# Four edits in one two-block kernel: head sums in one-pass form, tail by token halves, table rows on two queues, filter taps ahead of splits

## The chip, the cores and the metric

One Trainium2 chip, one core. The metric is device time in microseconds (us) of one execution of the whole program. The profiled execution is one more run of the same program with the hardware profiler on.

## The reference, cut to what matters

Two blocks are applied to x, 256 tokens of 2048 channels, all in float32. The first has two layers of attention plus spatial gating, and a convolution-gated feed-forward part. The second block (`second_block`) modulates by a conditioning vector and mixes the tokens in two branches: a long convolution (Hyena) and a state-space scan (SSD). It ends with a squared-ReLU MLP and a final norm. The pieces that the change touches are these.

```python
# filter of the long convolution, per channel and order
h = h * jnp.exp(-t[:, :, None, None] * jnp.abs(deltas))
k = jnp.concatenate([h[:, :, 0], zeros, h[:0:-1, :, 1]], axis=0)
k = k / (jnp.sum(jnp.abs(k), axis=0, keepdims=True) + EPS)
return jnp.fft.rfft(k, axis=0)

# within a chunk of 128 tokens, per head (16 heads, two directions)
cs = jnp.cumsum(a, axis=-1)
diff = cs[..., :, None] - cs[..., None, :]          # segsum, lower triangle
cb = jnp.einsum('bclgn,bcsgn->bgcls', cc, bc)
y_diag = jnp.einsum('bgcls,bgrcls,bcsgrp->bclgrp', cb, jnp.exp(segsum(a)), xdt)

# the end of the program
x = x + g2 * (jnp.square(jax.nn.relu(h @ w1)) @ w2)
return x * lax.rsqrt(jnp.mean(x * x, axis=-1, keepdims=True) + EPS) * final_norm_w
```

## The kernel before, in words

The core's time is a long row of products of 256 tokens with weights that stream from HBM. A weight piece is four tiles of 128x512. SP loads it in two halves into one of four slots (`w_raw`). ScalarE rounds it to float32r (`w_hi`, a form that TensorE takes in one pass), VectorE forms the remainder (`w_lo`), and TensorE runs three matmuls for each tile and token half: high by high, high by low, low by high. All five engines run orders written out by hand. What sets them against each other are semaphores: `w_loaded`, `w_hi`, `w_lo` and `w_free` for the slots, `t_full` and `t_free` for the two PSUM banks `turn0` and `turn1`, `side_full` and `side_free` for the banks `side0` and `side1`, `acc_free` for the four accumulator banks.

**Start.** Before the first product the per-channel vectors of layer 0 must be turned into columns. `table_rows(0)` names nine DMAs of rows into `staged`: two of 16 rows, three of 8 rows, then `conv_b` and three of `conv_w` of 88 rows each. ScalarE's queue issues all of them (L908), behind three for `cond_rows` (L904, L905), and TensorE's `turn_tables` waits for all nine. SP meanwhile issues `ident`, the first quarter of x and the first weight pieces. TensorE turns two quarters of x (`turn_x`) before the first product.

**Filters.** The filter of the long convolution is made in eight steps, `FLT_A` and `FLT_B` giving the slots (a slot is one weight piece of the second block). In slot FLT_A[s] TensorE writes the raw filter to the side banks. VectorE then runs `filter_taps(s)` one slot later, in `filter_step`, after `split_lo2(n + 2)`, the remainder for the piece two slots ahead, or after the `ada_last` sums (`c_sums`) where that piece is one of `w_ada`. TensorE, at the end of its slot FLT_B[s], waits for `flt_taps` and writes the norm (L2600) and the transform (L2605). `filter_spectrum(s)` on VectorE reads them. SP stores the result with two DMAs into `k_store`, and the taps of the next step wait for these (`k_stored`). The step s = 1 lies in the loop ahead of the slots, s = 0 too.

**Heads.** For each of the 16 heads VectorE's `head_steps` scales masks by the step sizes into `dlh` (four instructions). TensorE's `head_sums` multiplies `dlh` as stationary operand with a triangle of `masks` as moving operand: four float32 matmuls of 128 columns for each of two directions. ScalarE exponentiates each direction (L1217, in a loop), VectorE multiplies by `cbm` (L1973), and TensorE's `head_outputs` runs six small matmuls (L2685). TensorE's order is sums of head h + 1, outputs of head h, sums of head h + 2, and so on, with two buffers of each kind.

**Tail.** In the last quarter of the MLP, `gated_add(1, p, c)` adds the gated product of column quarter c to x, ScalarE's `x_squares2` sums its squares. After the last quarter come `x_norm`, a root on GpSimd, eight multiplications by root and weight (L2172) and eight DMAs to `out` on SP's queue.

The instructions for one matmul slot are these:

```python
nc.tensor.matmul(o, h_[:, kt, tok], wh[:, k, 0:cols], start=(kt == first), stop=False)
nc.tensor.matmul(o, h_[:, kt, tok], wl[:, k, 0:cols], start=False, stop=False)
last = nc.tensor.matmul(o, l_[:, kt, tok], wh[:, k, 0:cols], start=False, stop=(kt == final))
```

## Time and profile before

| what | value |
|---|---|
| device time, median of 3 runs | 3502.82 us (3501.29 to 3503.66) |
| the profiled execution's own time | 3501.27 us |
| its span in the trace | 3499.5 us |
| TensorE busy (PE) | 3407.4 us, 97% |
| VectorE busy (DVE) | 2373.2 us, 68% |
| ScalarE busy (ACT) | 1618.5 us, 46% |
| mean granted TensorE clock | 0.991 of full |
| HBM read | 689.15 MB, 199 GB/s over the span |

Busy shares are averages over stages. TensorE is nearly always busy, so a stage's time is TensorE's own work plus the places where it waits. PE rows are matmul records, PEld rows are weight loads. A plain float32 matmul leaves two records, a float32r one leaves one. The printed length of a record holds its way through the array, so that neighbours overlap; the distance of two starts is the better price. SPq and ACTq rows are the issue of DMAs on these queues.

### The profile page before, as it was taken

How to read it: one execution, taken by the hardware profiler on the slowest of the kernel's cores; microseconds unless marked ns; L12 is line 12 of the kernel's file. 1: busy time of each engine (PE TensorE's matmuls, PEld its weight loads, DVE VectorE, ACT ScalarE, POOL GpSimd, SP SyncE). 2: the span in 40 equal slices, each digit the busy share in tenths (PEclk: the TensorE clock that was granted, in tenths of full speed). 3: DMA queues.
4: the chain of work that ended last, by engine and by line, in shares of the span. 5: the costliest groups of instructions: out<-in, count | busy, mean ns of one | idle time of the engine just before them, and what ended most of it. 6: DMA issues, size and time to landing. Idle time of an engine off the chain costs nothing.

```text
span 3499.5 us, 43122 instructions
## 1 busy us (share of the span) xinstructions
PE 3407.4 (97%) x15842; PEld 2805.7 (80%) x15842; DVE 2373.2 (68%) x2974; ACT 1618.5 (46%) x2146; POOL 32.5 (1%) x28
## 2 busy tenths in 40 slices
PE   8999999999999999999999999999999999999998
PEld 6888888887778888888887887777866788888886
DVE  5667888888666666777777676676676655556565
ACT  5555555455334555555555444234432544444443
POOL 0000000000000000000000000000000000000000
PEclk9999999999999999999999999999999999999999
DMA  7557777776677557777777773346603566666664
GB/s 256 147 178 222 222 224 228 228 223 217 223 227 222 150 177 220 223 228 232 233 229 239 256 247 113 101 150 198 216 19 127 168 215 207 210 207 214 200 221 156
DMA packets 369459, 697.56 MB, mean 199 GB/s; under 512 B 25487, under 2 KB 37792, under 8 KB 368672
## 3 DMA queue, kind: packets, MB, share of 16 engines
q1 hardware_dynamic: 368628, 695.25, 62.9%
q8 instruction: 101, 1.65, 0.2%
q14 instruction: 46, 0.38, 0.0%
q10 hardware_dynamic: 684, 0.28, 0.0%
HBM read 689.15 MB, written 6.29 MB: 199 GB/s over the span
## 4 chain that ended last, share of the span: by engine, by line
PE 64%; issue 22%; DVE 6%; DMA 3%; ACT 2%; DVEq 2%; ACTq 0%; POOL 0%; SPq 0%; POOLq 0%
PE acc L2185 16%; PE acc L2187 16%; PE acc L2186 16%; PE acc L2473 3%; PE acc L2475 3%; PE acc L2474 3%; DMA w_raw<-in_w_down 2%; DVE w_lo L1320 2%; PE turn L2395 1%; DVE ada_sum L1424 1%; PE turn L2206 1%; PE turn L2222 1%; ACT w_hi L825 1%; DVEq L1416 1%; PE acc L2685 1%
## 5 line engine op out<-in xcount | busy, mean ns | idle before, releaser
L1320 DVE TENSOR_TENSOR w_lo<-w_raw,w_hi 128x1024 fp32r<-128x1024 f32 x708 | 838.4, 1221 | 372.9 <-ACT w_hi L825 336.2
L825 ACT ACTIVATE w_hi<-w_raw 128x1024 fp32r<-128x1024 f32 x708 | 739.0, 1062 | 718.2 <-DMA w_raw<-in_w_up 317.4
L2185 PE MATMUL acc<-w_hi,in_h 128*128 128x512 f32 x1408 | 552.7, 393 | 0.0
L2187 PE MATMUL acc<-w_hi,in_l 128*128 128x512 f32 x1408 | 548.6, 390 | 0.0
L2186 PE MATMUL acc<-w_lo,in_h 128*128 128x512 f32 x1408 | 548.1, 389 | 0.0
L2124 DVE TENSOR_TENSOR w_lo<-w_raw,w_hi 128x1024 fp32r<-128x1024 f32 x252 | 303.4, 1223 | 196.1 <-ACT w_hi L1284 186.3
L1284 ACT ACTIVATE w_hi<-w_raw 128x1024 fp32r<-128x1024 f32 x252 | 265.0, 1060 | 332.2 <-DMA w_raw<-in_w_mlp 331.6
L2473 PE MATMUL acc<-w_hi,in_h 128*128 128x512 f32 x992 | 394.7, 398 | 8.4 <-DVE in_l L2100 4.3
L2474 PE MATMUL acc<-w_lo,in_h 128*128 128x512 f32 x992 | 388.3, 391 | 0.8 <-issue 0.8
L2475 PE MATMUL acc<-w_hi,in_l 128*128 128x512 f32 x992 | 388.5, 392 | 0.0
L1424 DVE SCALAR_TENSOR_TENSOR ada_sum<-w_raw,silu_c,ada_sum 128x512 f32<-128x512 f32 x450 | 327.6, 750 | 31.0 <-issue 7.0
L2185 PEld LDWEIGHTS acc<-w_hi,in_h 128*128 128x128 f32 x1408 | 264.4, 188 | 56.0 <-issue 1.7
L2187 PEld LDWEIGHTS acc<-w_hi,in_l 128*128 128x128 f32 x1408 | 264.3, 188 | 55.3
L2186 PEld LDWEIGHTS acc<-w_lo,in_h 128*128 128x128 f32 x1408 | 264.5, 188 | 53.4
L2185 PE MATMUL acc<-w_hi,ah 128*128 128x512 f32 x704 | 279.5, 397 | 14.5 <-DVE w_lo L1320 8.5
L2187 PE MATMUL acc<-w_hi,al 128*128 128x512 f32 x704 | 276.6, 393 | 0.0
L2186 PE MATMUL acc<-w_lo,ah 128*128 128x512 f32 x704 | 276.4, 393 | 0.0
L2473 PEld LDWEIGHTS acc<-w_hi,in_h 128*128 128x128 f32 x992 | 187.7, 189 | 49.9 <-issue 11.2
L2475 PEld LDWEIGHTS acc<-w_hi,in_l 128*128 128x128 f32 x992 | 187.5, 189 | 41.1 <-issue 1.2
L2474 PEld LDWEIGHTS acc<-w_lo,in_h 128*128 128x128 f32 x992 | 187.6, 189 | 38.1 <-issue 0.7
L2473 PE MATMUL acc<-w_hi,hid_h 128*128 128x512 f32 x512 | 200.3, 391 | 0.0
L2475 PE MATMUL acc<-w_hi,hid_l 128*128 128x512 f32 x512 | 199.3, 389 | 0.0
(365 smaller groups left out, 4714.6 us busy)
## 6 DMA issues: line engine op xcount, KB each, us to landing
w_raw<-in_w_up SPq DMA_DIRECT2D x352, 512.0 KB, 3.8
w_raw<-in_w_mlp SPq DMA_DIRECT2D x256, 512.0 KB, 3.7
w_raw<-in_w_in SPq DMA_DIRECT2D x200, 512.0 KB, 3.7
w_raw<-in_w_ada SPq DMA_DIRECT2D x192, 512.0 KB, 4.2
w_raw<-in_w_down SPq DMA_DIRECT2D x176, 512.0 KB, 5.0
w_raw<-in_w_o SPq DMA_DIRECT2D x64, 512.0 KB, 3.7
w_raw<-in_w_out SPq DMA_DIRECT2D x32, 512.0 KB, 3.9
K<-k_store SPq DMA_DIRECT2D x16, 256.0 KB, 6.5
```

The costliest lines, as they stand in the source:

```text
L825: nc.scalar.activation(hi[s][:, ks], raw[s][:, ks], ACT.Copy).then_inc(w_hi[s][h], 1)
L1284: nc.scalar.activation(hi[s][:, 2 * h:2 * h + 2], raw[s][:, 2 * h:2 * h + 2], ACT.Copy).then_inc(w_hi[s][h], 1)
L1320: nc.vector.tensor_tensor(lo[s][:, ks], raw[s][:, ks], hi[s][:, ks].bitcast(F32), ALU.subtract).then_inc(w_lo[s][h], 1)
L1416: dve.drain()
L1424: a = nc.vector.scalar_tensor_tensor(ada_sum[v][:], raw[s][:, k], c, ada_sum[v][:], ALU.mult, ALU.add)
L2124: nc.vector.tensor_tensor(lo[s][:, ks], raw[s][:, ks], hi[s][:, ks].bitcast(F32), ALU.subtract).then_inc(w_lo[s][h], 1)
L2185: nc.tensor.matmul(acc[p][i][:], high(kt)[:, tok], hi[s][:, k], start=(kt == first), stop=False)
L2186: nc.tensor.matmul(acc[p][i][:], high(kt)[:, tok], lo[s][:, k], start=False, stop=False)
L2187: last = nc.tensor.matmul(acc[p][i][:], low(kt)[:, tok], hi[s][:, k], start=False, stop=(kt == final))
L2473: nc.tensor.matmul(o, h_[:, kt, tok], wh[:, k, 0:cols], start=(kt == first), stop=False)
L2474: nc.tensor.matmul(o, h_[:, kt, tok], wl[:, k, 0:cols], start=False, stop=False)
L2475: last = nc.tensor.matmul(o, l_[:, kt, tok], wh[:, k, 0:cols], start=False, stop=(kt == final))
```

## The change

It has four parts.

1. **Table rows on two queues.** SP issues the last four of the nine table DMAs, behind `ident` and ahead of x, once `staged` is cleared. ScalarE's queue keeps the first five.
2. **Filter taps ahead of splits.** `filter_step` falls in two: `filter_first` (the taps) runs ahead of `split_lo2` or of the `ada_last` sums of its slot, `filter_second` (the spectrum) where both stood.
3. **Heads.** The triangle is the stationary operand and the scaled mask moves. All are float32r: the step sizes are split once into `da_h` and `da_l`, VectorE makes `dlh` from `da_h`, ScalarE makes `dll` from `da_l` (four more activations for each head, `low_steps`). Each direction takes two matmuls of 384 columns and two of 128. ScalarE's loop over heads is written out, and three masks are copied to float32r (`masks_r`).
4. **Tail.** The last two pieces of the MLP run for token half 0 first and then for half 1 (`last_rows`). Each half has its own add, square sum, root and output. Columns 0 to 1535 are multiplied by the norm weight beforehand (`x_g`); ScalarE applies the root to part of them and issues two of the output DMAs on its own queue.

```diff
@@ constants
-    c["masks"] = np.stack([k <= q, k > q, k + q >= 0, k < q, k >= q], 1).astype(f32)
+    c["masks"] = np.stack([k <= q, k + q >= 0, k >= q, k > q, k < q], 1).astype(f32)
@@ buffers
-    dlh = [sbt(f"dlh{i}", [P, 2, 3 * P], at=at(3 * i)) for i in range(2)]
+    dlh = [sbt(f"dlh{i}", [P, 2, 3 * P], F32R, at(3 * i)) for i in range(2)]
+    dll = [sbt(f"dll{i}", [P, 2, 3 * P], F32R, at(24 + 3 * i)) for i in range(2)]
...
@@ sync
         sp.dma_start(ident[:], t["ident"]).then_inc(ident_in, 16)
+        sp.wait_ge(staged_clear, 1)
+        for dst, src in table_rows(0)[5:]:
+            sp.dma_start(dst, src).then_inc(staged_in, 16)
         x_chunk(0)
...
-        for i in range(TT):
-            for c in range(4):
-                sp.wait_ge(final_s, 4 * i + c + 1)
-                sp.dma_start(out[0, i * P:(i + 1) * P, c * CH:(c + 1) * CH], x_sb[:, i, c * CH:(c + 1) * CH]).then_inc(stored, 16)
+        for i, c in ((0, 3), (0, 0), (0, 1), (0, 2), (1, 3), (1, 2)):
+            sp.wait_ge(*(((final_a, c + 1) if i == 0 and c < 3 else (final_s, (1 if i == 0 else 5 - c)))))
+            src = x_sb[:, i, c * CH:(c + 1) * CH] if c == 3 else x_g[:, i, c * CH:(c + 1) * CH]
+            sp.dma_start(out[0, i * P:(i + 1) * P, c * CH:(c + 1) * CH], src).then_inc(stored, 16)
@@ gpsimd
-        root(22, x_rstd[:], x_ss[:], TT)
+        for i in range(TT):
+            root(22 + i, x_rstd[:, i:i + 1], x_ss[:, i:i + 1], 1)
@@ scalar
-        for dst, src in table_rows(0):
+        for dst, src in table_rows(0)[:5]:
...
+                    act_.wait_ge(dft_in, 48)
+                    for i, m in enumerate((1, 3, 4)):
+                        a = nc.scalar.activation(masks_r[:, i], masks[:, m], ACT.Copy)
+                    a.then_inc(masks_s, 1)
...
-        for g in range(2):
-            with act_.Fori(0, 4) as hp:
-                for m in range(2):
-                    h = act_.snap(hp * 2 + (8 * g + m))
...
+        def low_steps(h, m):
+            step = lambda i, d: da_l[:, i, ds(h + d * NH, 1)].bitcast(F32)
+            nc.scalar.activation(dll[m][:, 0, 0:2 * P], masks[:, LE:ONES + 1].rearrange("p m q -> p (m q)"), ACT.Copy, scale=step(0, 0))
+            nc.scalar.activation(dll[m][:, 0, 2 * P:], masks[:, LE], ACT.Copy, scale=step(1, 0))
+            nc.scalar.activation(dll[m][:, 1, 0:2 * P], masks[:, ONES:GE + 1].rearrange("p m q -> p (m q)"), ACT.Copy, scale=step(1, 1))
+            nc.scalar.activation(dll[m][:, 1, 2 * P:], masks[:, GE], ACT.Copy, scale=step(0, 1)).then_inc(dll_s, 1)
...
+        for m in range(2):
+            low_steps(m, m)
+        for h in range(NH):
+            exponentials2(h, h % 2)
+            if h + 2 < NH:
+                low_steps(h + 2, h % 2)
...
+        for i in range(TT):
+            act_.wait_ge(x_up, 8 + i)
+            square_sum2(x_sb[:, i, 3 * CH:], x_parts[:, i, 3:4]).then_inc(x_sq, 1)
+            act_.wait_ge(gained_s, 3)
+            act_.wait_ge(rstd, 22 + i)
+            for c in range((3, 2)[i]):
+                ch = slice(c * CH, (c + 1) * CH)
+                nc.scalar.activation(x_g[:, i, ch], x_g[:, i, ch], ACT.Copy, scale=x_rstd[:, i:i + 1]).then_inc(final_a, 1)
+                if i == 1:
+                    act_.wait_ge(final_a, 4 + c)
+                    nc.scalar.dma_start(out[0, P:, ch], x_g[:, 1, ch]).then_inc(stored, 16)
@@ vector
+            nc.vector.tensor_copy(da_h[:], dt_da[:])
+            dve.drain()
+            nc.vector.tensor_tensor(da_l[:], dt_da[:], da_h[:].bitcast(F32), ALU.subtract)
...
         for j in range(12):
             for n, s in pieces_of(j):
+                if n > 0:
+                    filter_first(n)
                 if n + 2 in ADA2:
...
                 if n > 0:
-                    filter_step(n)
+                    filter_second(n)
...
+                if last and n in (20, 24, 29):
+                    c = (n - 20) // 4
...
+                    nc.vector.tensor_tensor(x_g[:, :, ch], x_sb[:, :, ch], f_norm[:, ch].unsqueeze(1).to_broadcast([P, TT, CH]), ALU.mult).then_inc(gained_s, 1)
...
+        for i in range(TT):
+            dve.wait_ge(rows_done, i + 1)
+            nc.vector.tensor_tensor(res_t[1][:, i], acc[1][i][:], g_rows[1][:, ch], ALU.mult)
+            dve.drain()
+            nc.vector.tensor_tensor(x_sb[:, i, ch], x_sb[:, i, ch], res_t[1][:, i], ALU.add).then_inc(x_up, 1)
+            dve.wait_ge(x_sq, 63 + i)
+            nc.vector.tensor_reduce(x_ss[:, i:i + 1], x_parts[:, i], X_AXIS, ALU.add)
...
+            dve.wait_ge(rstd, 22 + i)
+            nc.vector.scalar_tensor_tensor(x_sb[:, i, ch], x_sb[:, i, ch], x_rstd[:, i:i + 1], f_norm[:, ch], ALU.mult, ALU.mult).then_inc(final_s, 1)
+        nc.vector.tensor_scalar(x_g[:, 1, 2 * CH:], x_g[:, 1, 2 * CH:], x_rstd[:, 1:2], None, ALU.mult).then_inc(final_s, 1)
@@ tensor, head_sums
-                own = ((0, 0), (2 * P, P)) if d == 0 else ((P, 0), (2 * P, 2 * P))
-                across = P if d == 0 else 0
-                for at_, l0 in own:
-                    nc.tensor.matmul(tb[b][:, at_:at_ + P], w[:, d, l0:l0 + P], masks[:, near], start=True, stop=True)
-                part = 2 * P if d == 0 else P
-                nc.tensor.matmul(tb[b][:, across:across + P], w[:, d, 0:P], masks[:, ONES], start=True, stop=False)
-                last = nc.tensor.matmul(tb[b][:, across:across + P], w[:, d, part:part + P], masks[:, near], start=False, stop=True)
+                across = (P, 0)[d]
+                for w in (dlh[m], dll[m]):
+                    nc.tensor.matmul(tb[b][:, 0:3 * P], masks_r[:, 1 + d], w[:, d], start=(w is dlh[m]), stop=False)
+                for w in (dlh[m], dll[m]):
+                    last = nc.tensor.matmul(tb[b][:, across:across + P], masks_r[:, 0], w[:, d, 2 * P:], start=False, stop=(w is dll[m]))
@@ tensor
+        def last_rows(p):
+            for i in range(TT):
+                tok = slice(i * P, (i + 1) * P)
+                for n in (30, 31):
...
+                last.then_inc(rows_done, 1)
```

Three places in the order of the instructions. The first is VectorE in slot 13, the last filter step, where the piece two slots ahead is one of `w_ada`. Before:

```order
L1408 SCALAR_TENSOR_TENSOR ada_last_156<-w_raw_59,silu_c,ada_last_156 128x512 [waits w_loaded3_1]
L1408 SCALAR_TENSOR_TENSOR ada_last_156<-w_raw_59,silu_c,ada_last_156 128x512
L1844 TENSOR_TENSOR flt_h_199<-side,flt_decay 128x512 [waits side_full1,side_full0]
L1845 SCALAR_TENSOR_TENSOR flt_q<-side,not_first_sb,flt_decay 128x256
L1846 TENSOR_TENSOR flt_q<-side,flt_decay 128x256
L1850 TENSOR_TENSOR flt_sum<-flt_h_199,flt_q 128x512 [waits k_stored]
```

And now:

```order
L1898 TENSOR_TENSOR flt_sum<-flt_h_204,flt_q 128x512 [waits k_stored]
L1899 TENSOR_TENSOR flt_dif<-flt_q,flt_h_204 128x512
L1901 TENSOR_TENSOR flt_q<-flt_sum,flt_dif 128x512
L1902 TENSOR_TENSOR flt_h_204<-flt_sum,flt_dif 128x512
L1904 SCALAR_TENSOR_TENSOR flt_q<-flt_h_204,flt_q 128x512
L1449 TENSOR_SCALAR ada_last_156<-w_raw_59,silu_c 128x512 [waits w_loaded3_0]
L1451 SCALAR_TENSOR_TENSOR ada_last_156<-w_raw_59,silu_c,ada_last_156 128x512
L1451 SCALAR_TENSOR_TENSOR ada_last_156<-w_raw_59,silu_c,ada_last_156 128x512 [waits w_loaded3_1]
L1451 SCALAR_TENSOR_TENSOR ada_last_156<-w_raw_59,silu_c,ada_last_156 128x512
L1911 TENSOR_SCALAR flt_r<-turn 128x256 [waits t_full1]
```

The taps moved ahead of the four sums, and the four sums now stand between taps and spectrum.

The second is ScalarE in the heads. Before, a pass of the loop is one load of the exponential table and two heads (the numbers behind the names are buffers):

```order
L1217 ACT_TABLE_LOAD
L1217 ACTIVATE decays_196<-turn 128x384 [waits t_full0]
L1217 ACTIVATE decays_196<-turn 128x384 [waits t_full1]
L1215 REGISTER_ALU
L1216 REGISTER_ALU [waits mt_used]
```

And now, two heads in a row:

```order
L1239 ACTIVATE decays_202<-turn 128x384 [waits t_full0,mt_used]
L1239 ACTIVATE decays_202<-turn 128x384 [waits t_full1]
L1227 ACTIVATE dll_197<-masks_sb,da_l 128x256
L1228 ACTIVATE dll_197<-masks_sb,da_l 128x128
L1229 ACTIVATE dll_197<-masks_sb,da_l 128x256
L1230 ACTIVATE dll_197<-masks_sb,da_l 128x128
L1239 ACTIVATE decays_201<-turn 128x384 [waits t_full0,mt_used]
```

Four activations from SBUF came in between the exponentials of one head and of the next, and the table is loaded once.

The third is the end of ScalarE's order, where nothing but the square sums stood before:

```order
L1133 ACTIVATE junk_242,x_parts<-x_sb 128x512 [waits x_up]
L1351 ACTIVATE x_g<-x_g,x_rstd 128x512 [waits rstd,gained_s]
L1354 DMA out<-x_g 128x512 [waits final_a]
L1351 ACTIVATE x_g<-x_g,x_rstd 128x512
L1354 DMA out<-x_g 128x512 [waits final_a]
```

These are the rows of token half 1: a square sum, and two copies with a DMA issue behind each.

## Rows read from the trace of the kernel before

**Rows 1.** TensorE's longest wait: in total, times, longest, us
```profile
PE turn L2600 <- DVEq L1857: 11.7, 6, 3.8
```

**Rows 2.** Timeline of the start: start us, us, engine, what, idle before
```profile
5.34 1.40 ACTq L908 DMA_DIRECT2D staged<-in_conv_w x3
...
13.72 1.30 PE L2206 MATMUL turn<-ident_sb,staged 128*128 128x128 f32 x5 [4.92 <-DMA staged<-in_conv_w]
...
20.09 0.77 PE L2185 MATMUL acc<-w_hi,n_h 128*128 128x512 f32 x1
```

**Rows 3.** DMA issues in the first 45 us: KB each, median us to landing
```profile
ident_sb<-in_ident SPq DMA_DIRECT2D x1, 64.0 KB, 1.8
...
cond_rows<-in_b_ada ACTq DMA_DIRECT2D x1, 48.0 KB, 5.9
```

**Rows 4.** DMA issues from 2.6 to 3.1 us: the second quarter of x
```profile
x_sb<-in_x SPq DMA_DIRECT2D x1, 512.0 KB, 8.0
```

**Rows 5.** Timeline of TensorE at the filter steps
```profile
2210.61 1.13 PE L2600 MATMUL turn<-flt_q,masks_sb 128*128 128x256 f32 x4 [0.66 <-DVEq L1857]
...
2268.75 2.07 PE L2600 MATMUL turn<-flt_q,masks_sb 128*128 128x256 f32 x4 [3.54 <-DVEq L1857]
...
2320.71 1.13 PE L2600 MATMUL turn<-flt_q,masks_sb 128*128 128x256 f32 x4 [1.47 <-DVEq L1857]
...
2325.66 0.40 PE L2504 MATMUL side<-ident_sb,dt_T 32*128 32x32 f32 x4 [2.08 <-DVE flt_h L1869]
```

**Rows 6.** Timeline of VectorE at the filter steps, slots 9 and 13
```profile
2261.11 2.35 DVE L1759 TENSOR_TENSOR w_lo<-w_raw,w_hi 128x1024 fp32r<-128x1024 f32 x2
...
2311.69 0.48 DVE L1406 TENSOR_SCALAR ada_last<-w_raw,silu_c 128x512 f32<-128x512 f32 x1 [8.13 <-PE acc L2491]
...
2317.20 0.69 DVE L1850 TENSOR_TENSOR flt_sum<-flt_h,flt_q 128x512 f32<-128x512 f32 x1 [0.62 <-DMA k_store<-flt_dif]
```

**Rows 7.** Windows: length, busy PE, PEld, DVE, ACT, POOL, then granted clock, DMA
```profile
2261.00:2272.00 11.00, 7.46 (x33) 6.13 (x32) 8.11 (x13) 0.00 (x0) 0.00 (x0) 0.84 0.45 132
...
2531.30:2579.00 47.70, 47.54 (x424) 47.25 (x423) 28.06 (x72) 19.93 (x38) 0.00 (x0) 1.00 0.17 58
```

**Rows 8.** Timeline of TensorE in the heads
```profile
2549.25 1.45 PE L2685 MATMUL acc<-xdt,decays 128*128 x12
...
2550.54 0.66 PE L2672 MATMUL turn<-masks_sb,dlh 128*128 128x128 f32 x4
...
2552.38 1.45 PE L2685 MATMUL acc<-xdt,decays 128*128 x12
```

**Rows 9.** Timeline of TensorE: float32r matmuls of 256 columns in a row
```profile
2288.12 0.28 PE L2475 MATMUL acc<-w_hi,hc_l 128*128 128x256 f32 x1
2288.24 0.28 PE L2473 MATMUL acc<-w_hi,hc_h 128*128 128x256 f32 x1
```

**Rows 10.** Windows: the last 11 us of TensorE, 512 columns each
```profile
3475.00:3486.00 11.00, 10.96 (x49) 8.74 (x47) 1.81 (x3) 0.00 (x0) 0.00 (x0) 1.00 0.00 0
```

**Rows 11.** Groups of instructions: one by form, xcount, busy us, mean ns
```profile
L1272 ACT ACTIVATE in_h<-n_f,mod 128x256 fp32r<-128x256 f32 x16 | 7.2, 500 | 5.4 <-DVE n_f L2109 5.4
```

**Rows 12.** Timeline of ScalarE behind the heads
```profile
2577.59 0.49 ACT L1217 ACTIVATE decays<-turn 128x384 f32<-128x384 f32 x1 [0.40 <-PE turn L2675]
2577.98 2.43 ACT L1220 ACTIVATE g_diag<-ident_sb,mod 128x128 f32<-128x128 f32 x8
```

**Rows 13.** Timeline of the tail
```profile
3486.00 1.29 DVE L2081 TENSOR_TENSOR res_t<-acc,g_rows 128x512 f32<-128x512 f32 x2 [9.19 <-PE acc L2475]
...
3488.63 0.63 ACT L1123 ACTIVATE junk<-x_sb 128x512 f32<-128x512 f32 x1 [16.25 <-DVE x_sb L2084]
...
3491.40 5.39 DVE L2172 SCALAR_TENSOR_TENSOR x_sb<-x_sb,x_rstd,f_norm 128x512 f32<-128x512 f32 x8 [0.81 <-POOL x_rstd L794]
...
3492.18 4.97 SPq L785 DMA_DIRECT2D out<-x_sb x8
```

**Rows 14.** DMA issues in the last 10 us: KB each, us to landing
```profile
out<-x_sb SPq DMA_DIRECT2D x8, 256.0 KB, 2.2
```

More of the change, by code:

```diff
@@ L1296, in hidden @@
                     a.then_inc(acc_free[p], 1)
-                if last and n >= 16 and n % NS == 3:
+                if last and n >= 16 and n % NS == 3 and n < 31:
                     x_squares2(4 + (n - 16) // NS + 1, (n - 16) // NS)
@@ L1946, in _ @@
         block_scales((2,))
-        LE, GT, ONES, LT, GE = range(5)
+        LE, ONES, GE, GT, LT = range(5)
         for g in range(2):
@@ L2135, in hidden @@
                         sl, r = ring(mlp_product(n), q)
-                        dve.wait_ge(w_free[sl][1], r + 1)
-                        if last:
+                        if not (last and c == 3):
+                            dve.wait_ge(w_free[sl][1], r + 1)
+                        if last and c < 3:
                             gated_add(1, p, c)
+                        elif last:
+                            continue
                         else:
@@ L2686, in head_outputs @@
             last.then_inc(mt_used, 1)
+        pe.wait_ge(masks_s, 1)
         head_sums(0, 0)
@@ L2791, in _ @@
         last.then_inc(side_full[0], 1)
+        def last_rows(p):
+            for i in range(TT):
+                tok = slice(i * P, (i + 1) * P)
+                for n in (30, 31):
+                    s, r = ring(mlp_product(n), 3)
+                    for k in range(4):
+                        kt = 4 * (n - 28) + k
+                        if k % 2 == 0:
+                            pe.wait_ge(w_lo[s][k // 2], r)
+                        nc.tensor.matmul(acc[p][i][:], hid_h[:, kt, tok], hi[s][:, k], start=False, stop=False)
+                        nc.tensor.matmul(acc[p][i][:], hid_h[:, kt, tok], lo[s][:, k], start=False, stop=False)
+                        last = nc.tensor.matmul(acc[p][i][:], hid_l[:, kt, tok], hi[s][:, k], start=False, stop=(kt == KT - 1))
+                last.then_inc(rows_done, 1)
         def hidden(q, last_q):
@@ L2823, in hidden @@
                     n = 16 + NS * c + s
+                    if last_q and n >= 30:
+                        if n == 30:
+                            last_rows(p)
+                        continue
                     product2(mlp_product(n), 4 * s, [(p, hid_h, hid_l, CH)], q)
```

55 lines of the change are left out of this document (35 added, 20 removed).

## The prediction, made before the changed kernel had run

> **What bounds the kernel now.** I read the waits of TensorE first, then the timelines around each of them, then the windows for the granted clock. TensorE works nearly all of the span, so an edit pays only where it shortens TensorE's own work or a wait of TensorE, or what lies before its first and after its last product. The four parts of the change sit at four such places. At the start nothing can be multiplied before nine rows of tables have landed [rows 2]. At the filter steps TensorE waits six times for VectorE's taps [rows 1, 5]. In the heads TensorE is full, and its records are short [rows 8]. After the last product 13.5 us pass, from 3486.0 to the end of the span at 3499.5 [rows 13]. The rest of the kernel, some 3,350 us of products, keeps its instructions and should take what it took.
>
> **Start.** The last table DMAs are issued on ScalarE's queue from 5.34 to 6.74; TensorE turns the rows at 13.72, and the first product starts at 20.09, 6.4 us behind [rows 2]. So the rows land some 7 us after their issue, where `ident`, first in its queue and alone, took 1.8 us and `b_ada`, issued at about 2.2 behind three large loads on SP, took 5.9 [rows 3]. In the changed kernel SP issues the four rows of 88 first, from about 1.9 (the memset of `staged`) to 3.7, so they land before its large loads start. What is left on ScalarE's queue ends with a DMA that was issued at 4.6. Priced like `b_ada`, which had as many large loads ahead of it, it lands at 10.5; priced like `ident`, at 6.4. I take 9.5, nearer to `b_ada`: 4.2 us sooner. The price is that all of SP's loads start 2.5 us later (four issues and the wait). The second quarter of x landed at 2.71 + 8.0 = 10.7 [rows 4] and will at 13.2; TensorE turns it 4.3 us behind the tables, at 13.8, so it just hides. If the tables came sooner still, this quarter would be late next, and the gain ends at 5 us.
>
> The Trainium skill, "DMA: Bandwidth & Descriptors", section "Issuing engines are not separate DMA queues", speaks against this: starting DMAs from several engines saves only the time of issuing them. Here the time of issue is 1.8 us (the last DMA of ScalarE's queue ends at 5.0 in place of 6.74), and by the rule that would be the gain. No row shows a queue with the rows ahead of the large loads.
>
> **Filter taps.** The taps take 5.3 us (from the end of two remainders at 2263.4 to TensorE's start at 2268.75) and the two remainders ahead of them 2.3 us [rows 5, 6]. Six waits come to 11.7 us [rows 1]. Two of them, 1.7 and 3.8 us, belong to the steps ahead of the slots, whose order stays. The four others are 0.66 in slot 5, 3.54 in slot 9, a like one of 0.6 in slot 11, and 1.47 in slot 13 [rows 5]. With the taps 2.3 us earlier the small ones go (1.2 us) and slot 9 keeps 1.3, because there VectorE comes late from the convolution taps: 2.3 us off. In slot 13 nothing is gained: the taps stood still for the store into `k_store` until 2317.20 [rows 6], a DMA that SP issues when TensorE has finished its slot, so they end at 2320.6 as before. And something is lost: the four `ada_last` sums, 3.2 us from 2311.69 [rows 6], ran while TensorE wrote the raw filter and the store was under way. Now they stand between the taps and the spectrum, start at 2320.7 and end at 2323.9, where the spectrum started at 2321.9. TensorE's wait for the spectrum's second product grows from 2.1 to 4.1 us [rows 5]. Net: 1.2 + 2.3 - 2.0 = 1.5 us. After the wait of 3.54 us the granted clock was down for a while (0.84 over that window) [rows 7]; the record behind it takes 2.07 us for what takes 1.13 elsewhere [rows 5]. If that goes it gives another 0.16 x 11 = 1.8 us, of which some may come back in slot 13, so I take 1.2. Together 2.7 us, between a loss of 1 (the clock falls in slot 13 and still in slot 9) and a gain of 4. The remainders that now stand behind the taps are for two slots later and are hidden by at least one product.
>
> **Heads.** One head takes 3.13 us, the distance of two groups of outputs [rows 8], and TensorE is busy in 47.54 of 47.70 us [rows 7]. That is 28 records, 16 for the sums and 12 for the outputs, at 0.112 us each. The sums become four records of 384 columns and four of 128. A float32r record of 256 columns takes 0.12 us [rows 9], one of 512 takes 11.0 / 49 = 0.225 [rows 10]; half way is 0.172. For 128 columns in one pass no row stands; below it is a quarter of 0.225, 0.056, above it the 0.12 of 256 columns, and I take 0.112, since the output records, with half as many columns as the sums, take the same, so it is the weights that set it. Sums: 4 x 0.172 + 4 x 0.112 = 1.14 in place of 1.79. The head would be 2.48 us.
>
> The Trainium skill, "TensorE: Matmul & The Clock Gate", section "Weight-path perf modes — Fast Weight Load (FWL) and DoubleRow", says that fast weight load is on for 128 weights of a type that is not FP32; if float32r counts so, the short records cost 0.056 and TensorE needs 2.25 us a head. No run here shows it.
>
> ScalarE gets four activations for each head. Two exponentials of 0.49 and, from the diagonals behind them, 0.30 for one of 128 columns (eight in 2.43) [rows 12]; for 256 columns 7.2 / 16 = 0.45 [rows 11]. That makes 1.0 + 0.6 + 0.9 = 2.5 us, level with TensorE. So the head settles at about 2.5 us, and 15 of them save 15 x 0.63 = 9.4. The first head's sums run at the lower clock and save 1.0 more; the last head's outputs wait a little longer for VectorE (0.2). 10.2 us in all. Lower bound: copies at their full printed length, 0.50 and 0.39, with the exponentials and some 0.15 of handover make 2.9 a head, 4 us saved. Upper bound: ScalarE at 2.3, 13 us. VectorE's part keeps its size and stays hidden (28.06 of 47.70 us busy [rows 7]); the split of the step sizes and the three masks lie in slots with idle VectorE and ScalarE and cost nothing; if their cover went, it would be 2 us.
>
> **Tail.** Token half 0 is done 5.4 us before the last product, and its sum, root and four stores hide under half 1. For half 1 the chain from 3486.00 to the first final multiplication at 3491.40 shrinks: one product instead of two (0.6 less), an add of half the size (0.5 less), one square sum instead of two (0.8 less) [rows 13], so 3489.5. Then ScalarE copies 0.6, issues 0.45, copies 0.6 and issues at 3491.4, where SP's last of eight issues began at about 3496.6 [rows 13]. A store lands 2.2 us behind its issue [rows 14]. The end comes 5.2 us sooner, between 4 and 6. The second half of piece 31 is needed 2.7 us earlier; its remainder was ready at 3476.8, and it is needed at 3479.
>
> **The sum.** 4.2 + 2.7 + 10.2 + 5.2 = 22.3 us. The profiled execution took 3501.27 (span 3499.5), so 3479.0; the median of the runs is 1.55 above that execution, and the median of the changed kernel should be 3502.82 - 22.3 = **3480.5**. A measurement of this kernel tells 0.2%, some 7 us, from no change.
>
> **Rivals.**
> - *ScalarE becomes the bound of the heads.* For it: the copies stand between two exponentials of different heads, and the sum of its printed lengths is 2.9 us. Against it: neighbours overlap in every row of it. The heads then save 4 in place of 10.2: 3486.7.
> - *The two queues save only their issue.* 1.8 in place of 4.2, if the rows on ScalarE's queue still stand behind SP's loads. For it: the skill's rule above, which gives just this, and `b_ada`'s 5.9 us with no large DMA of its own queue ahead. Against it: the large loads now come behind the long rows. 3482.9.
> - *Slower: the lower clock in the heads.* If TensorE waits for ScalarE in every head and the chip grants the lower of its two clocks, 1.2 in place of 2.4 GHz, a head takes 2 x 2.48 = 4.96, 29 us more over 16 heads in place of 10 fewer: 3502.8 + 29 - 12.1 = 3520. It decides from the point where the clock is down in about six of ten heads. For it: the clock was down after single waits of 2 to 4 us. Against it: the waits here would be tenths of a us, and in the heads before the clock was full throughout [rows 7].
> - *The taps gain nothing* and slot 13 costs 2 us and a fall of the clock: 3484. This is in the range.
>
> **How the numbers follow.** The forecast, each part near its term, 0.70; ScalarE as the bound 0.13; only the issue saved 0.12; the lower clock or another loss 0.03; the rest, that a part does nothing, 0.02. The range takes in the first three with their bounds, all lows together being rare: 3473 to 3489. Faster by more than 0.2% are all but the lower clock and half of the rest: 0.96; same 0.01, slower 0.03.
>
> **What would show it.** Start: first table transposes at about 9.5 and first product at about 16. Filter: the waits of slots 5 and 11 gone, about 1.3 in slot 9, over 3.5 for L2504's successor in slot 13, `ada_last` behind the taps. Heads: groups of outputs 2.5 apart, one table load, short records at 0.112. Tail: 8 us in place of 13.5 between the last product and the end. The prediction is wrong if the head period stays over 2.8 us, if the tables are turned after 12, or if the products between these places change their time.

## The result, and the profile after

The changed kernel takes 3518.85 us (median of 6 runs, 3516.13 to 3520.45), the kernel before 3502.06 in the same comparison (6 runs). The ratio is 1.0044, with a 95% interval of 1.0033 to 1.0054. So it is 17 us **slower**, where 22 us faster was forecast. That is the time of the third rival (3520), which I had given 3 in 100.

The page of the changed kernel, its span, TensorE and ScalarE, and the granted clock in 40 slices of 88 us:

```profile
span 3518.0 us, 42928 instructions
PE 3434.2 (98%) x15714; PEld 2833.1 (81%) x15714; DVE 2373.9 (67%) x2977; ACT 1641.2 (47%) x2215; POOL 33.0 (1%) x29
PEclk9999999999999999999999999999869999999999
```

TensorE is busy for 27 us more with 128 records fewer, and two slices of the clock stand out, the 29th and the 30th. The heads are there. The windows of the entry to the heads, of 40 us inside them, and of their end (columns as in [rows 7]):

```profile
2520.00:2525.00 5.00, 3.75 (x21) 2.99 (x19) 2.06 (x11) 3.83 (x10) 0.00 (x0) 1.00 0.48 143
2525.00:2530.00 5.00, 2.39 (x9) 2.23 (x10) 2.71 (x13) 2.31 (x4) 0.00 (x0) 0.73 0.92 279
...
2600.00:2605.00 5.00, 5.00 (x16) 3.65 (x16) 0.41 (x1) 0.48 (x2) 0.00 (x0) 0.50 0.00 0
2605.00:2610.00 5.00, 3.21 (x7) 0.99 (x6) 3.92 (x7) 0.00 (x0) 0.00 (x0) 0.92 0.00 0
```

```profile
2533.00:2573.00 40.00, 40.00 (x172) 40.00 (x173) 16.53 (x45) 19.67 (x51) 0.00 (x0) 0.50 0.12 37
```

The granted clock is 0.50, the lower of the two levels (1.2 GHz), from about 2527 to about 2605, although TensorE works without a gap. In the same heads before it was 1.00 [rows 7]. Two heads on TensorE's timeline:

```profile
2553.01 0.67 PE L2738 MATMUL turn<-dlh,masks_r 128*128 128x384 f32 x1
2553.47 0.52 PE L2738 MATMUL turn<-dll,masks_r 128*128 128x384 f32 x1
2553.79 0.31 PE L2740 MATMUL turn<-dlh,masks_r 128*128 128x128 f32 x1
...
2555.18 2.76 PE L2750 MATMUL acc<-xdt,decays 128*128 x12
2557.70 0.67 PE L2738 MATMUL turn<-dlh,masks_r 128*128 128x384 f32 x1
```

A head takes 4.69 us (2553.01 to 2557.70), before 3.13 [rows 8].

There is a second, shorter wait at the entry, ahead of the sums of head 1, where the kernel before has none:

```profile
2529.52 0.69 PE L2738 MATMUL turn<-dlh,masks_r 128*128 128x384 f32 x1 [0.85 <-ACT decays L1239]
```

It is for ScalarE, which loads its exponential table (1.28 us, from 2527.68) only when the first sums of head 0 are there. Before the change that load began at 2523.77, ahead of these sums.

The other three places, TensorE and the engines it waits for. First the start, which answers to [rows 2]:

```profile
9.50 1.30 PE L2274 MATMUL turn<-ident_sb,staged 128*128 128x128 f32 x5 [4.76 <-DMA staged<-in_b_s]
...
13.79 1.94 PE L2274 MATMUL turn<-ident_sb,x_sb 128*128 128x128 f32 x8 [1.16 <-DVE n_l L1372]
...
15.86 0.77 PE L2253 MATMUL acc<-w_hi,n_h 128*128 128x512 f32 x1
```

Then the filter steps, which answer to [rows 5] (slots 5, 9, 11 and 13, and dt's turn behind slot 13), and VectorE in slot 13, as in [rows 6]:

```profile
2205.42 1.02 PE L2668 MATMUL turn<-flt_q,masks_sb 128*128 128x256 f32 x4
2262.45 1.13 PE L2668 MATMUL turn<-flt_q,masks_sb 128*128 128x256 f32 x4 [0.92 <-DVEq L1905]
2285.79 1.03 PE L2668 MATMUL turn<-flt_q,masks_sb 128*128 128x256 f32 x4
2313.40 1.13 PE L2668 MATMUL turn<-flt_q,masks_sb 128*128 128x256 f32 x4 [1.42 <-DVEq L1905]
2320.62 0.60 PE L2572 MATMUL side<-ident_sb,dt_T 32*128 32x32 f32 x4 [4.36 <-DVE flt_h L1917]
```

```profile
2309.88 0.69 DVE L1898 TENSOR_TENSOR flt_sum<-flt_h,flt_q 128x512 f32<-128x512 f32 x1 [2.02 <-DMA k_store<-flt_dif]
...
2315.02 1.57 DVE L1451 SCALAR_TENSOR_TENSOR ada_last<-w_raw,silu_c,ada_last 128x512 f32<-128x512 f32 x2 [0.26 <-issue]
2316.84 0.42 DVE L1911 TENSOR_SCALAR flt_r<-turn 128x256 f32<-128x256 f32 x1 [0.25 <-issue]
```

And the tail, which answers to [rows 13] (the last product ends at 3509.4):

```profile
3509.40 0.69 DVE L2231 TENSOR_TENSOR res_t<-acc,g_rows 128x512 f32<-128x512 f32 x1 [1.39 <-PE acc L2871]
...
3514.69 0.37 ACTq L1354 DMA_DIRECT2D out<-x_g  x1
```

How far ahead of the kernel before the changed one is, at marks that both have:

| mark | before | after | ahead |
|---|---|---|---|
| first product | 20.09 | 15.86 | 4.2 |
| norm of slot 5 | 2210.61 | 2205.42 | 5.2 |
| norm of slot 11 | 2294.25 | 2285.79 | 8.5 |
| norm of slot 13 | 2320.71 | 2313.40 | 7.3 |
| dt's turn | 2325.66 | 2320.62 | 5.0 |
| turn of `cvC` in slot 16 | 2367.45 | 2365.87 | 1.6 |
| first sums of head 0 | 2528.33 | 2526.76 | 1.6 |
| first product behind the heads | 2580.59 | 2602.53 | -21.9 |
| end of the last product | 3486.0 | 3509.4 | -23.4 |
| end of the span | 3499.5 | 3518.0 | -18.5 |

The heads lose 23.5 us, and 1.5 more are lost behind them, while the clock comes back. The slots lose 6.9 us of the 8.5 between the norm of slot 11 and slot 16. The tail gives 4.9.

### The profile page after: what moved, and what is told of

Same layout as the page of the kernel before. It is cut to its first block, busy times and chain, and to the rows that moved or that the text cites. A ratio compares the mean times of both kernels' runs of the same rounds, so it can differ in the third digit from the quotient of the medians.

```text
span 3518.0 us, 42928 instructions
## 1 busy us (share of the span) xinstructions
PE 3434.2 (98%) x15714; PEld 2833.1 (81%) x15714; DVE 2373.9 (67%) x2977; ACT 1641.2 (47%) x2215; POOL 33.0 (1%) x29
## 4 chain that ended last, share of the span: by engine, by line
PE 86%; DVE 6%; ACT 2%; DMA 2%; DVEq 2%; issue 1%; ACTq 0%; POOL 0%; SPq 0%; POOLq 0%
PE acc L2253 16%; PE acc L2255 16%; PE acc L2254 16%; PE acc L2541 9%; PE acc L2543 9%; PE acc L2542 9%; DMA w_raw<-in_w_down 2%; DVE w_lo L1363 1%; PE acc L2750 1%; PE turn L2463 1%; PE turn L2274 1%; PE turn L2290 1%; DVE ada_sum L1467 1%; PE turn L2738 1%; DVEq L1459 1%
```

## The experiments

### Which part loses: heads alone, and all but the heads

`e1_without_heads` is the changed kernel with its third part taken back (the masks' order, `dlh` in float32, `head_sums`, ScalarE's loop, the split of the step sizes). `e2_heads_alone` is the kernel before with that part alone.

> The changed kernel with its heads put back as they were before (triangle moving, float32, the loop on ScalarE); start, taps and tail stay changed. Theory A, the heads carry the whole loss: they gave 25.1 us away and the split of the step sizes about 1.4 more in slot 15, so this kernel is at 3518.9 - 26.5 = 3492, 10 us faster than before, and the granted clock in the heads is full from 2531 on. Rival B, the other three parts pull the clock of the heads down too (they come sooner, other waits ahead of them): it stays near 3517.

> The kernel before with the heads alone changed. Theory A: 3502 + 25 + 1 = 3528, the granted clock at 0.50 in all 16 heads, 4.7 us a head. Rival B, it needs the other parts as well: the heads take 2.5 us each at the full clock and the kernel is at 3492.

Measured: without the heads 3492.0 us (9 runs, 3486.8 to 3499.3; ratio 0.9965, 0.9955 to 0.9975); the heads alone 3528.5 (4 runs, 3527.8 to 3536.0; ratio 1.0068, 1.0051 to 1.0084). The windows of each inside its heads (for the heads alone, from the run of 3536.0):

```profile
2533.00:2563.00 30.00, 30.00 (x271) 30.00 (x271) 18.73 (x50) 11.75 (x21) 0.00 (x0) 1.00 0.10 32
```

```profile
2545.00:2600.00 55.00, 55.00 (x236) 55.00 (x236) 22.61 (x60) 27.47 (x71) 0.00 (x0) 0.50 0.08 25
```

Both stand where theory A put them. The third part costs 3518.85 - 3492.0 = 27 us, and needs no help from the other parts. One thing in the first of them is not as expected: its old heads stand behind the same wait of TensorE (2.61 us), and yet the granted clock of the profiled execution is 1.00 from 2521 on. So such a wait does not always bring a fall.

### The entry or the mix: dense work ahead of the heads

In front of head 0 TensorE stood idle, in both kernels, for VectorE, which made the group products in `cbm` (2.4 us) and then the four masks of the step sizes (1.0 us): 2.66 us now, 2.61 before. The clock fell there in both. The windows of the kernel before:

```profile
2525.00:2530.00 5.00, 2.39 (x12) 1.96 (x11) 4.28 (x20) 0.05 (x1) 0.00 (x0) 0.79 0.84 239
2530.00:2535.00 5.00, 5.00 (x39) 4.85 (x39) 2.60 (x6) 1.96 (x4) 0.00 (x0) 0.87 1.07 379
2535.00:2540.00 5.00, 5.00 (x47) 5.00 (x47) 2.94 (x10) 2.75 (x4) 0.00 (x0) 1.00 0.84 267
```

There it was back within some 3.4 us (0.21 of 5 us and 0.13 of 5 us missing, at half speed); in the changed kernel it wasn't. Is it that the changed records can't bring the clock back, or that they can't keep it?

```diff
         pe.wait_ge(masks_s, 1)
+        b0, k0 = UNITS["E", 0, 0]
+        pe.wait_ge(t_free[b0], k0)
+        for _ in range(36):
+            nc.tensor.matmul(tb[b0][:, 0:3 * P], masks_r[:, 1], masks_r[:].rearrange("p m q -> p (m q)"), start=True, stop=True)
         head_sums(0, 0)
```

> The changed kernel with 36 more float32r matmuls of 384 columns in the gap ahead of the first head, so that TensorE is at its full clock when the heads begin. They are extra work: their result is overwritten. Theory E, only the fall at the entry matters and the heads keep a clock that is full: 40 us of heads at 2.5 us each, 33 us less than the changed kernel and 4 us more for the extra matmuls, so about 3490. Theory M, the mix of records in the heads cannot hold the full clock: it falls again within a few heads and the time is 3518 to 3523.

Measured: 3485.2 us (2 runs, 3484.4 and 3485.9), 5 us under what I had put. TensorE in the heads, and the window of 30 us there:

```profile
2534.91 0.42 PE L2738 MATMUL turn<-dlh,masks_r 128*128 128x384 f32 x1
...
2536.09 1.50 PE L2750 MATMUL acc<-xdt,decays 128*128 x12
2537.39 0.42 PE L2738 MATMUL turn<-dlh,masks_r 128*128 128x384 f32 x1
```

```profile
2533.00:2563.00 30.00, 30.00 (x244) 30.00 (x243) 22.94 (x63) 28.59 (x74) 0.00 (x0) 1.00 0.06 18
```

Theory E holds. With the same instructions in the heads a head takes 2.48 us at a granted clock of 1.00, and it stays there for all 16. Only the level at which TensorE enters is different. ScalarE is busy 28.59 of 30 us, 2.36 a head, and TensorE does not wait for it in this window. It does ahead of head 1: there it waited 1.35 us for ScalarE's table load and exponentials, and the clock stayed full.

`e11_pause` asks the same from the other side. On the same kernel VectorE copies `cbm` onto itself three times ahead of head 8.

> The kernel with 36 extra matmuls (3485.2, full clock in all heads) and one pause ahead of head 8: VectorE copies the group products onto themselves three times, about 5 us, and TensorE waits some 3 to 4 us for it. If one fall is enough for the rest of the heads, heads 8 to 15 run at 0.50 and 4.7 us each, so 3485 + 4 + 8 x 2.2 + 2 = 3509. If the mix of the heads can raise the clock again, it is back after some us and the time is 3485 + 4 + 2 = 3491.

```profile
2551.72 0.44 PE L2742 MATMUL turn<-dlh,masks_r 128*128 128x384 f32 x1 [2.29 <-DVE dlh L2018]
```

```profile
2533.00:2548.00 15.00, 15.00 (x124) 15.00 (x123) 11.42 (x29) 14.24 (x37) 0.00 (x0) 1.00 0.05 17
2556.00:2576.00 20.00, 20.00 (x86) 20.00 (x86) 7.55 (x21) 9.44 (x24) 0.00 (x0) 0.50 0.00 0
```

TensorE waited 2.29 us, once, and the rest of the heads ran at 0.50. No second wait stands behind it, so the one ahead of head 1 in the changed kernel isn't needed to keep the clock down. The median of 8 runs is 3503.5, nearer to the 3509 of the first outcome than to 3491. It is 18.3 us over the kernel without the pause, of which TensorE was idle for 2.3: six of them carry the same loss (3502.5 to 3506.2), one took 3508.3, and one 3487.1. In that one the mean granted clock was 0.991, as without the pause, against 0.984 to 0.986, so the pause passed there without a fall that lasted.

`e4_extra_columns` leaves the entry as it is and issues the first sum record of each direction twice:

```diff
+                nc.tensor.matmul(tb[b][:, 0:3 * P], masks_r[:, 1 + d], dlh[m][:, d], start=True, stop=True)
                 for w in (dlh[m], dll[m]):
```

> The changed kernel with the first sum record of each direction (384 columns) issued twice; the first result is overwritten. Two more long records for each head, 22 in place of 20, or 768 more columns. Theory M, the records hold too few columns for their weight loads to bring the clock back: if these suffice, the clock is up from the second head on, a head takes 2.5 + 2 x 0.17 = 2.8 us and the kernel is at about 3492; if they don't suffice, the clock stays at 0.50, a head takes 4.7 + 2 x 0.32 = 5.3 us and the kernel is at 3529. Theory E (only the entry matters): 3529 as well.

```profile
2535.00:2540.00 5.00, 5.00 (x22) 5.00 (x22) 1.54 (x5) 2.02 (x6) 0.00 (x0) 0.50 0.58 185
2540.00:2545.00 5.00, 5.00 (x24) 5.00 (x24) 1.54 (x6) 2.02 (x7) 0.00 (x0) 0.54 0.00 0
2545.00:2550.00 5.00, 5.00 (x41) 5.00 (x40) 3.24 (x10) 3.62 (x11) 0.00 (x0) 1.00 0.00 0
```

3496.5 us (8 runs, 3493.7 to 3500.8; ratio 0.9982, 0.9971 to 0.9992). More work, and 22 us less time. The clock fell at the entry and came back some 17 us later. It came later than I had put it (the second head), so the time is 4 us over the 3492 of theory M. Whether the columns or the number of the records did it, no run here separates. Together the four kernels say: the changed heads keep the full clock when they have it, and don't win it back when they have lost it; with two more records of 384 columns for each head they do.

### What the entry needs

`e5_dense_15` has 15 of the extra matmuls in place of 36. `e6_steps_ahead` has none. It makes the gap smaller: the masks of heads 0 and 1 come ahead of VectorE's last modulation and of `cbm`, ScalarE makes `dll` of head 0 ahead of its silu, VectorE that of head 1, and TensorE runs the sums of head 0 ahead of the eight float32 group products.

```diff
-        last_modulation(ADA_BLOCK + 1)
-        block_scales((2,))
...
+        sl, r = ring(pieces_of(11)[-1][0])
+        dve.wait_ge(w_free[sl][1], r + 1)
         head_steps(0, 0)
+        last_modulation(ADA_BLOCK + 1)
+        block_scales((2,))
+        low_steps_v(1, 1)
+        head_steps(1, 1)
```

> The changed kernel with 15 extra matmuls of 384 columns in the gap ahead of the first head, in place of 36: they take 15 x 0.173 = 2.6 us, just the gap. If TensorE's activity in the gap is what keeps the clock full, the kernel is at 3485.2 or slightly under it (the 36 ended at about 2526.9, when head 0's steps were ready, and cost hardly anything). If 15 leave too little, the clock falls as in the changed kernel and it is at 3517.

> No extra work: the gap itself is taken away. The step masks of heads 0 and 1 are made before VectorE's last modulation and the group products, ScalarE makes the low part of head 0 ahead of its silu, and TensorE runs the sums of head 0 ahead of the group products. The first outputs start some 4 us sooner than in the kernel with 36 extra matmuls and TensorE has no gap over 1.5 us. If the clock stays full: 3485.2 - 4 = 3481. If the clock falls at the entry all the same: 3514.

Measured: 3482.3 (3 runs, 3479.4 to 3483.5) and 3484.0 (4 runs, 3480.6 to 3485.4). With 15 the sums of head 0 start at 2523.0, against 2526.9 with 36, so the 36 weren't as cheap as I had written: the medians are 2.9 us apart. The wait ahead of head 1 stands there too, and the clock stayed full behind it:

```profile
2525.73 0.44 PE L2738 MATMUL turn<-dlh,masks_r 128*128 128x384 f32 x1 [1.34 <-ACT decays L1239]
```

In `e6_steps_ahead` the wait for `dll`, 1.00 us, ended at 2523.4. The clock fell at about 2524.3, in the sums of head 0, and was back 3.4 us later, while the group products ran:

```profile
2522.50:2525.00 2.50, 1.58 (x9) 1.61 (x10) 2.27 (x11) 2.37 (x5) 0.00 (x0) 0.87 0.75 218
2525.00:2527.50 2.50, 2.50 (x7) 1.96 (x8) 0.65 (x4) 2.49 (x7) 0.00 (x0) 0.50 0.90 272
2527.50:2530.00 2.50, 2.21 (x15) 2.02 (x13) 2.17 (x8) 1.45 (x5) 0.00 (x0) 0.95 0.97 297
```

At half speed that is 1.7 of the 3 us by which it missed 3481, and since the clock came back it is no 3514 either.

### The slots

On the kernel with 36 extra matmuls `e7_slots` issues the store of filter step 6 one piece sooner on SP's queue and moves the split of the step sizes out of slot 15:

```diff
-                if n == max(3, FLT_B[s] + 5):
+                if n == max(3, FLT_B[s] + (4 if s == 6 else 5)):
                     filter_store(s)
```

> The kernel with 36 extra matmuls, and two edits in the slots: the store of step 6 is issued one piece sooner on SP's queue, and the split of the step sizes (two VectorE instructions) moves from slot 15 to chunk 11. The store: the taps of slot 13 no longer stand still, so the wait of 1.4 us ahead of the norm goes and the one ahead of the product behind it falls from 4.4 to about 2; with the lower clock behind them 2.3 to 3 us. The split: the wait of 1.34 us for a remainder in slot 15 goes, 1.3 to 2.6 us. Together 3485.2 - 5 = 3480. If the losses in the slots came from the taps standing ahead as such, it stays at 3485.

Measured: 3484.2 (4 runs, 3479.5 to 3486.7), which the spread of the runs doesn't tell from 3485.2. The profile does, between two marks. From the norm of slot 11 (2286.47) to the turn of `cvC` (2361.62) it takes 75.2 us, 80.1 in the changed kernel. The wait ahead of the norm of slot 13 is gone; the one for a remainder in slot 15 fell from 1.34 to 0.5. The wait ahead of dt's turn only fell from 4.4 to 4.1:

```profile
2319.39 0.40 PE L2572 MATMUL side<-ident_sb,dt_T 32*128 32x32 f32 x4 [4.12 <-DVE flt_h L1912]
```

So the store was worth 1.9 us up to dt's turn (32.9 us from the norm of slot 11, 34.8 in the changed kernel), under the 2.3 to 3 expected. What stands between taps and spectrum are the four sums. Two more kernels, on the one with 15 matmuls, move these sums in slot 13 alone: ahead of the taps, as before the change, and behind the spectrum. The edit of the first:

```diff
-                if n > 0:
+                if n > 0 and n != 13:
                     filter_first(n)
...
+                if n == 13:
+                    filter_first(n)
                 if (j, s) == (SHARED, 1):
```

> The kernel with 15 extra matmuls (3482.3), the store of step 6 sooner, the split of the step sizes in chunk 11, and in slot 13 alone the four ada_last sums ahead of the taps, as before the change. From the norm of slot 11 to the turn of slot 16's convolution it took 73.2 us before the change, 80.1 in the changed kernel and 75.2 with the store and the split mended. If the sums between taps and spectrum are what is left of the loss, the wait ahead of dt's turn falls from 4.1 to 2.1 us, a wait of about 1.5 stands ahead of the norm, the stretch takes 72 to 74 us and the kernel is at 3477 to 3480. If it was the phase of the clock, the stretch stays at 75 or more and the time at 3482.

> The same with the four ada_last sums of slot 13 behind both, taps and spectrum. No wait ahead of the norm, 2 us ahead of dt's turn, but the convolution taps and remainders behind the sums come 3.3 us later. If VectorE has that much slack in slot 14, the stretch takes 71 to 73 us and the kernel is at 3476 to 3479; if not, TensorE waits for a remainder in slot 14 or 15 for up to 3 us, the clock falls again and it is no better than the kernel with the sums first.

In the profiled executions the stretch takes 73.1 us with the sums first (waits of 0.9 and 2.1) and 74.3 with the sums last (2.1 ahead of dt's turn, and 2.3 for a remainder, the second outcome that I had named). The kernels with the same slots that follow show how far such a number can be trusted:

```profile
2284.86:2357.99 73.13, 67.30 (x359) 56.26 (x357) 54.25 (x91) 31.08 (x47) 0.00 (x0) 0.95 0.53 163
2283.96:2353.92 69.96, 64.11 (x358) 53.98 (x357) 54.34 (x91) 31.08 (x47) 0.00 (x0) 1.00 0.54 170
```

The first line is this stretch with the sums first, the second the same stretch in `e12_slots_dense_36`, with the same instructions and the same waits (in `e13_slots_steps_ahead` it takes 69.96 us too). In the first the clock fell twice, in the second not at all: 3.2 us between two executions that differ in nothing else here. So the 1.2 us between 73.1 and 74.3 rank neither order above the other.

The times are another story. With the sums last: 3479.9 (5 runs, 3477.1 to 3482.5). With the sums first the median of 3507.4 says nothing, since the 12 runs fall into two groups: 3473.8 to 3477.5 (5 runs, mean granted clock 0.991 to 0.993) and 3506.9 to 3515.6 (7 runs, 0.980 to 0.982). The profiled execution is of the slower group:

```profile
2521.69 0.44 PE L2740 MATMUL turn<-dlh,masks_r 128*128 128x384 f32 x1 [1.35 <-ACT decays L1239]
```

```profile
2533.00:2563.00 30.00, 30.00 (x131) 30.00 (x130) 12.51 (x33) 15.90 (x41) 0.00 (x0) 0.50 0.00 1
```

The clock fell at about 2522.2, just behind the wait for head 0's exponentials, with the table load in it, and stayed down for all the heads. The same wait of 1.34 to 1.35 us stands in the profiles of four kernels here that kept the full clock behind it (`e3_dense_entry`, `e5_dense_15`, `e10_slot13_sums_last`, `e12_slots_dense_36`), so it alone doesn't decide. The same program, the same chip, 35 us apart: 15 matmuls don't make it safe.

### Two versions that don't depend on it

> The kernel whose runs fell apart into 3474 to 3478 and 3507 to 3516 (sums first in slot 13, store sooner, split moved, 15 extra matmuls), with 36 extra matmuls in place of 15. If what decides is whether TensorE is dense for long enough when the clock is looked at near the entry, every run keeps the full clock in the heads and lies between 3474 and 3482, at a cost of at most 3 us against the fast group with 15. If the phase decides all the same, a part of the runs is again at 3507 or over.

> No extra matmuls: the same slots with the order in which the steps of heads 0 and 1 are made ahead and the float32 group products stand between the sums of heads 0 and 1. There the clock fell at the entry and was back 3.5 us later, while the group products ran. If such a piece of denser work behind the fall is enough, every run is at 3474 to 3480. If the fall can also come behind the group products, a part of the runs is at 3505 or over.

Measured: `e12_slots_dense_36` 3476.5 us (5 runs, 3472.3 to 3479.5; ratio 0.9926, 0.9913 to 0.9940); `e13_slots_steps_ahead` **3469.3 us** (4 runs, 3468.3 to 3472.6; ratio 0.9908, 0.9893 to 0.9923). No run of either is over 3480. The first is where it was expected, the second 5 us under its 3474: its first outputs of a head start 7.1 us sooner than the first's (2515.4 and 2522.5), since no extra matmuls stand ahead of them. With 5 and 4 runs, a rare lost clock can't be ruled out. The second does no extra work and beats both kernels, by 33 and by 50 us. The gap ahead of head 0 is down to 1.0 us, and in the profiled execution the clock doesn't fall between 2245 and the end of the heads:

```profile
2510.42 0.41 PE L2747 MATMUL turn<-dlh,masks_r 128*128 128x384 f32 x1 [1.00 <-ACT dll L1133]
...
2511.59 1.94 PE L2758 MATMUL side<-bcT 128*128 128x256 f32 x8
2513.18 0.53 PE L2747 MATMUL turn<-dlh,masks_r 128*128 128x384 f32 x1
```

```profile
2518.00:2548.00 30.00, 29.81 (x240) 29.68 (x239) 23.23 (x65) 28.08 (x73) 0.00 (x0) 1.00 0.23 76
```

### The start

`e8_rows_behind` is the kernel with 36 matmuls, with SP's four rows behind two quarters of x and the first weight piece.

> The kernel with 36 extra matmuls, and the four long rows on SP's queue moved behind the first quarter of x, the first weight piece and the second quarter of x. If the gain at the start came from the issues alone (two queues issue at once), the tables are turned within 0.5 us of 9.5 again, since the rows are still issued sooner than ScalarE's queue did before. If it came from the rows standing ahead of the large loads, they land late: tables turned at 12 to 13.5 and the first product 2.5 to 4 us later, 3488 to 3489.

```profile
11.11 1.30 PE L2275 MATMUL turn<-ident_sb,staged 128*128 128x128 f32 x5 [2.29 <-DMA staged<-in_conv_w]
...
17.47 0.77 PE L2254 MATMUL acc<-w_hi,n_h 128*128 128x512 f32 x1
```

Neither outcome holds: the tables are turned at 11.11, before the change at 13.72, in the changed kernel at 9.50. So 2.6 us of the gain come with two queues issuing (the last row is issued by 5.4 in place of 6.74) and 1.6 with the rows standing ahead of the large loads. The time is 3486.5 (3 runs, 3485.5 to 3488.9), 1.3 over the kernel with 36 matmuls, under the 3488 to 3489 of the second outcome.

## Why the prediction was wrong, point by point

- **Start: right.** Tables at 9.5 and first product at about 16; measured 9.50 and 15.86, 4.2 us gained as put down. The Trainium skill, "DMA: Bandwidth & Descriptors", section "Issuing engines are not separate DMA queues", lets one expect the saved issue time alone, which was 1.8 here. The traces disagree: 4.2 were gained, 2.6 even where the rows stood behind large loads. The 9.5 was a choice between 6.4 and 10.5 that no row fixed.
- **Filter taps: the terms were right, the clock was not.** Up to slot 11 the taps brought 4.2 us on top of the start (4.7 put down: 1.2 + 2.3 and 1.2 from the clock): the waits of slots 5 and 11 are gone, slot 9 keeps 0.92 where I had 1.3, and the clock didn't fall there. In slot 13 the sums between taps and spectrum cost 2.3 at dt's turn (2.0 put down). But 1.2 more went in slot 12: TensorE's wait of 2.3 us for `yB` is in both kernels, and only in the changed one the clock fell behind it. Behind dt's turn the clock took another 0.8, since it fell sooner. Without the third part (`e1_without_heads`) the kernel is 3.7 us ahead at its first product and 3.3 at the first sums of head 0: the taps by themselves are at -0.4, inside the range of -1 to 4 that I had given them, and far from the 2.7.
- **The failed step of the slots: "the split of the step sizes and the three masks lie in slots with idle VectorE and ScalarE and cost nothing; if their cover went, it would be 2 us".** In slot 15 the remainder of the next piece came 1.34 us late, TensorE waited, and the clock was down for twice as long as before (a granted clock of 0.66 over 2355 to 2365, so 6.8 of 10 us, against 3.4): 2.6 us. Not all of it is the split's. In `e1_without_heads`, which has no split and no masks, the same wait is 0.62 us, and from the last running sums to the turn of `cvC` it takes 8.8 us, against 10.7 in the changed kernel and 8.1 before. So split and masks cost 1.9 us by these two profiles, 0.7 of it in the wait and the rest at the lower clock, near the 2 named for lost cover; the other 0.7 is there without them. Moved to chunk 11, the split cost nothing that the profile shows. From the first product to the heads the second part, with the split, lost 2.6 us, where 2.7 were put down as gained.
- **Heads: the full-clock sum was right, and the level was wrong.** At the full clock a head takes 2.48 us, as forecast, but in part by luck: the four long records take 0.83 us together where 0.69 were put down, the four short ones 0.35 for 0.45 (0.06 and 0.11 in turn), the outputs 1.30 for 1.34. ScalarE takes 2.36 a head and holds TensorE up only once, ahead of head 1 (0.85 us in the changed kernel, 1.35 at the full clock), so the first rival is out. That one wait, for the table load, is in no term of the sum. What failed is the sentence "in the heads before the clock was full throughout" used as evidence against the third rival. The window I quoted began at 2531.3. Ahead of it the clock had fallen in the kernel before as well, and its records brought it back. The prediction knew of that fall: it lets "the first head's sums run at the lower clock" and counts 1.0 us for it. The step that failed is therefore not a price but the assumption, made without a row, that the changed records would bring the clock back behind these sums as the old ones did. In the sum it is +10.2 against a measured -25.0.
- **The third rival had the right level, the wrong trigger, and its number by luck.** 3520 against 3518.85: it put the heads at -29, which lost 25.0, and the other three parts at +12.1, which gave 6.5. I had it depend on TensorE waiting for ScalarE in every head, and judged it by that: waits of tenths of a microsecond. From the second head on TensorE didn't wait at all (72.00 of 72.00 us from 2530 to 2602). One wait of 2.66 us ahead of them was enough, in all 6 runs by their times. The 4.96 us that I took for a head at the lower clock was 4.69.
- **Tail: right.** 4.9 us for 5.2. The span ends 8.6 us behind the last product (13.5 before), and the last issue, on ScalarE's queue, comes 5.3 us behind it.
- **Sum.** 4.2 - 2.6 - 25.0 + 4.9 = -18.5, by which the spans differ. With the heads at the full clock and nothing else changed the forecast of 3480.5 would have been 3482 to 3485, as the kernels with 15 and 36 extra matmuls show; these matmuls and the slots are the rest.

The Trainium skill, "TensorE: Matmul & The Clock Gate", section "What's actually happening", has the clock fall behind an idle stretch and return when the engine is busy again. The first half agrees with the fall at the entry and with most others, but not with all: in slot 15 of the kernel before the clock fell with no wait of TensorE for 34 us, right behind 24 records of 16 columns (the running sums of the step sizes).

```profile
2357.67:2360.50 2.83, 2.83 (x26) 2.83 (x25) 2.75 (x6) 0.05 (x1) 0.00 (x0) 1.00 0.63 179
2360.50:2364.00 3.50, 3.50 (x9) 2.71 (x9) 3.16 (x4) 3.50 (x5) 0.00 (x0) 0.51 0.91 352
```

The second half doesn't agree either: from 2530 to 2602 the profile has TensorE busy in every microsecond, and the granted clock is 0.50. So TensorE's busy time in the profile does not tell its clock here.

## What to carry to other kernels

When a change makes a stretch of TensorE lighter (one pass in place of two, fewer columns behind each load of weights), look at the granted clock at its entry in the trace of before, not only inside it: a fall that the old records repaired in 3 us can last for the whole stretch with the new ones. If there is a wait of some microseconds ahead of such a stretch, close it with work that is due anyway, or put dense work between the wait and the stretch. And run it more than a few times: one kernel here had its runs 35 us apart, by whether the clock had fallen at one point.

## What was not expected of the hardware

- The same 20 records run at either level for as long as the stretch lasts: 2.48 us a head at 1.00, 4.69 at 0.50, in one program from run to run. What exactly decides between the two at the entry was not settled. A wait of 2.6 us passed without a fall in `e1_without_heads`, and one of 2.3 in one of the eight runs of `e11_pause`, by its time. By their times and mean clocks, all 22 runs of the five kernels with 36 extra matmuls kept the full clock at the entry, 13 of the 20 runs of the three with 15 did, and none of the 8 runs with the steps made ahead was lost, whether the clock fell at the entry (and came back under the float32 group products) or not.
- TensorE can be slower by being given less. Two extra records for each head, each only repeating work, made the kernel 22 us faster than the changed one (3496.5 and 3518.85).
- The ratio of the levels is not the ratio of the times, 4.69 to 2.48 being 1.89; for the outputs alone (12 records in 2.52 us and in 1.30) it is 1.94.
